# Six of 31 convolution taps as diagonal products on TensorE, compressors in column halves, and a new order of masks, Silus and one low part

## What is computed

```python
CONV_CH, CONV_WIDTH, SEQ = 256, 31, 256
N_Q_HEADS, N_KV_HEADS, HEAD_DIM = 12, 4, 64
CMP_LEN, CMP_STRIDE, CMP_HIDDEN = 32, 16, 256

def conv_mixer(a, w_dw, b_dw, ln_g, ln_b):
    u, v = jnp.split(a, 2, axis=-1)
    y = u * jax.nn.sigmoid(v)
    y = lax.conv_general_dilated(            # each channel alone, 31 taps, causal
        y, w_dw[:, None, :], window_strides=(1,),
        padding=[(CONV_WIDTH - 1, 0)],
        dimension_numbers=("NWC", "WIO", "NWC"),
        feature_group_count=CONV_CH) + b_dw
    y = layer_norm(y, ln_g, ln_b)
    return jax.nn.silu(y)

def compress(kr, pe, w1, w2):                # once for keys, once for values
    b, t = kr.shape[:2]
    chunks = kr.reshape(b, t // CMP_STRIDE, CMP_STRIDE, N_KV_HEADS, HEAD_DIM)
    lo = jnp.einsum("bclgd,ldh->bcgh", chunks, w1[:CMP_STRIDE])
    hi = jnp.einsum("bclgd,ldh->bcgh", chunks, w1[CMP_STRIDE:])
    h = lo[:, :-1] + hi[:, 1:] + jnp.einsum("ld,ldh->h", pe, w1)
    return jnp.einsum("bngh,hd->bngd", jax.nn.silu(h), w2)

def hybrid_layer(x, ...):
    h = rms_norm(x, attn_norm)
    z = h @ w_in                             # u v | q | kc vc ks vs kw vw | gates
    conv_out = conv_mixer(a_conv, conv_w, conv_b, conv_ln_g, conv_ln_b)
    kc = compress(kc_r, ...); vc = compress(vc_r, ...)
    nsa_out = nsa_attention(q, kc, vc, ks, vs, kw, vw, gates)
    x = x + concatenate([conv_out, nsa_out]) @ w_out
    ...                                      # feed-forward, then the second layer
```

## Time and profile before

| what | value |
|---|---|
| median of three executions | 749.86 us |
| the profiled execution: own time / span | 749.76 us / 748.0 us |
| PE busy in the span | 734.2 us (98%) |
| DVE / ACT / POOL busy | 538.5 us (72%) / 377.3 us (50%) / 51.0 us (7%) |
| TensorE clock granted, mean of the span | 0.996 |
| chain that ended last | PE 81%, DVE 12%, ACT 3%, DMA 2% |

### The profile page before, as it was taken

How to read it: one execution, slowest core, us unless ns; L and a number is a source line. 1 busy time by engine, 2 the same in 40 slices (tenths; PEclk the granted TensorE clock), 3 DMA queues, 4 the chain that set the end, 5 groups by cost and what they waited for, 6 DMA issues and landing times.

```text
span 748.0 us, 13134 instructions
## 1 busy us (share of the span) xinstructions
PE 734.2 (98%) x5288; PEld 677.4 (91%) x5288; DVE 538.5 (72%) x927; ACT 377.3 (50%) x544; POOL 51.0 (7%) x72
## 2 busy tenths in 40 slices
PE   8999999999999999999999999999999999999996
PEld 7999987789999999998999999999988998998995
DVE  6798798586677776847669978884967876555554
ACT  7533778664433334446444447665645444444442
POOL 1950000000000000000432000000000000000000
PEclk9999999999999999999999999999999999999999
DMA  8636421479787888642354556554733674644611
GB/s 329 236 117 238 161 65 50 161 307 340 285 317 298 304 323 318 233 161 93 131 195 151 175 198 254 202 188 170 270 124 113 248 258 170 224 168 168 224 57 57
DMA packets 27022, 151.10 MB, mean 202 GB/s; under 512 B 3128, under 2 KB 7836, under 8 KB 9564
## 3 DMA queue, kind: packets, MB, share of 16 engines
q1 hardware_dynamic: 22620, 124.81, 46.1%
q10 hardware_dynamic: 3456, 25.17, 8.5%
q0 software_dynamic: 896, 0.43, 0.3%
HBM read 148.92 MB, written 1.05 MB: 200 GB/s over the span
## 4 chain that ended last, share of the span: by engine, by line
PE 81%; DVE 12%; ACT 3%; DMA 2%; issue 1%; SPq 0%; DVEq 0%; ACTq 0%
PE ps L468 24%; PE ps L469 24%; PE ps L470 24%; DVE ada L1767 4%; DVE w_lo L1671 2%; PE ps L795 2%; PE ps L593 1%; DMA raw<-wts 1%; PE ps L1045 1%; ACT w_hi L1224 1%; DMA raw<-rows_b 1%; PE ps L627 1%; PE ps L617 1%; PE ps L645 1%; PE ps L1031 1%
## 5 line engine op out<-in xcount | busy, mean ns | idle before, releaser
L1671 DVE TENSOR_TENSOR w_lo<-raw,w_hi 128x2048 fp32r<-128x2048 f32 (+2 forms) x105 | 237.5, 2267 | 111.4 <-ACT w_hi L1224 111.1
L468 PE MATMUL ps<-h_hi,w_hi 128*128 128x256 f32 (+2 forms) x984 | 280.1, 285 | 0.0
L469 PE MATMUL ps<-h_lo,w_hi 128*128 128x256 f32 (+2 forms) x984 | 278.3, 283 | 0.0
L470 PE MATMUL ps<-h_hi,w_lo 128*128 128x256 f32 (+2 forms) x984 | 278.3, 283 | 0.0
L1224 ACT CAST w_hi<-raw 128x2048 fp32r<-128x2048 f32 (+2 forms) x105 | 196.8, 1886 | 50.4 <-PE ps L470 46.6
L468 PEld LDWEIGHTS ps<-h_hi,w_hi 128*128 128x128 f32 (+2 forms) x984 | 187.2, 190 | 2.1 <-issue 1.0
L469 PEld LDWEIGHTS ps<-h_lo,w_hi 128*128 128x128 f32 (+2 forms) x984 | 187.2, 190 | 1.2
L470 PEld LDWEIGHTS ps<-h_hi,w_lo 128*128 128x128 f32 (+2 forms) x984 | 187.2, 190 | 0.3
L468 PE MATMUL ps<-w_hi,mix_hi 128*128 128x512 f32 x248 | 97.5, 393 | 0.4 <-DVE w_lo L1671 0.2
L469 PE MATMUL ps<-w_lo,mix_hi 128*128 128x512 f32 x248 | 96.8, 390 | 0.0
L470 PE MATMUL ps<-w_hi,mix_lo 128*128 128x512 f32 x248 | 96.5, 389 | 0.0
(11 more groups left out here) (319 smaller groups left out, 920.2 us busy)
## 6 DMA issues: line engine op xcount, KB each, us to landing
raw<-wts SPq DMA_DIRECT2D x109, 1024.0 KB, 4.8
ada<-w_ada ACTq DMA_DIRECT2D x24, 1024.0 KB, 5.4
alibi<-wts SPq DMA_DIRECT2D x2, 1024.0 KB, 6.7
fa_whole<-wts SPq DMA_DIRECT2D x2, 1024.0 KB, 6.4
resid<-x SPq DMA_DIRECT2D x2, 512.0 KB, 3.8
raw<-wts SPq DMA_DIRECT2D x2, 512.0 KB, 6.8
rows_ga<-rows_wide SPq DMA_DIRECT2D x1, 1024.0 KB, 6.9
out<-resid SPq DMA_DIRECT2D x4, 256.0 KB, 2.0
```

Of the source, the lines that this page charges most:

```text
L468: nc.tensor.matmul(o, lh, rh, start=start, stop=False)
L469: nc.tensor.matmul(o, lh, rl, start=False, stop=False)
L470: return nc.tensor.matmul(o, ll, rh, start=False, stop=stop)
L1671: V.tensor_tensor(w_lo[:, s % RING, 0:w], raw[:, n_of[name] % RAW, 0:w], w_hi[:, s % RING, 0:w].bitcast(F32), ALU.subtract).then_inc(w_rea ...
```

## The change

The change has four parts.

1. The last six taps (25 to 30) of both channel tiles leave DVE. ACT makes twelve diagonal matrices (`tap_diag`: the identity times one column of tap weights, into `rows_ga`, which is free then) ahead of its first copy of a projection. PE multiplies them with the shifted `ypad` behind q1, into bank 7, twelve float32 products of 128 x 128 with 256 columns, and raises `tap_sum_ps`. DVE keeps 50 taps and adds the sum from PSUM to `conv` in one instruction, which now raises `conv_ready`. The taps behind each split are set by a table, 10, 10, 10, 8, 2, 10; the last ten stand behind the low part of vs.
2. A compressor's products are written as column halves: twice 64 columns of the weight block, into partitions 0 to 63 and 64 to 127 of the same PSUM columns, one half behind the other for each j.
3. On ACT the Silu of the keys goes ahead of the copy of the values' sums, and `after(7)`, the high part of vw, goes behind the Silu of the values. On DVE `masked(1)` goes ahead of the mean's subtraction.
4. On DVE `after(7)`, the low part of vw, goes from ahead of `compressor_sum(1)` to behind the copies of the compressed values, ahead of the reciprocal.

```diff
--- before.py
+++ after.py
@@ -82,6 +82,7 @@
 TILES = plan()
 STORED = memory_order()
 CMP_BASE = (0, 48)
+PE_TAPS = 6
 OWN_BANK = {"g": 7, "vs": 6, "vw": 7, "k1": 7}
 G_COLS = 36
 IDX_COLS = 136
@@ -171,6 +172,12 @@
         early = ada[:, :, :].rearrange("p a w -> p (a w)")
         ypad = early[:, 0:572].rearrange("p (c t) -> p c t", c=2)
         conv = early[:, 572:1084].rearrange("p (c t) -> p c t", c=2)
+        on_pe = [(w, c) for c in range(2) for w in range(CONV_W - PE_TAPS, CONV_W)]
+
+        def tap_diag(w, c):
+            i = on_pe.index((w, c))
+            return rows_ga[:, i // 8, (i % 8) * P:(i % 8 + 1) * P]
+
         lnv = early[:, 1084:1596].rearrange("p (a t) -> p a t", a=2)
         lnd = z[:, U, :].rearrange("p (c t) -> p c t", c=2)
         lnq = z[:, V_, :].rearrange("p (c t) -> p c t", c=2)
@@ -262,6 +269,7 @@
         dstep, astep, gstep = sem("dve_step"), sem("act_step"), sem("pool_step")
         zeroed, alibi_ready = sem("zeroed"), sem("alibi_ready")
         conv_ready, conv_mean, convd_ready, conv_var = (sem(n) for n in ("conv_ready", "conv_mean", "convd_ready", "conv_var"))
+        ypad_ready, diag_ready, tapsum_ps = (sem(n) for n in ("ypad_ready", "tap_diagonals_ready", "tap_sum_ps"))
         lnv_ready, lnsq_ready, lnn_ready, chi_ready, clo_ready = (sem(n) for n in (
             "lnv_ready", "lnsq_ready", "lnn_ready", "conv_hi_ready", "conv_lo_ready"))
         kr_ready, cmp_ps, cmp_sb, cmp_sum, cmp_h, cmp2_ps, cmp2_sb, vblk_ready = (sem(n) for n in (
@@ -580,6 +588,13 @@
             i.then_inc(pe_tile, 1)
             for s in range(1, 8):
                 feature_tile(*project_1(s), h_hi, h_lo, 0 if s == 1 else None).then_inc(pe_tile, 1)
+                if s == s_idx["q1"]:
+                    pe.wait_ge(ypad_ready, 1)
+                    pe.wait_ge(diag_ready, 2 * PE_TAPS)
+                    for w, c in on_pe:
+                        i = nc.tensor.matmul(ps[:, 7, c * T:(c + 1) * T], tap_diag(w, c), ypad[:, c, w:w + T],
+                                             start=(w == CONV_W - PE_TAPS), stop=(w == CONV_W - 1))
+                    i.then_inc(tapsum_ps, 1)
 
 
             def compress(a):
@@ -589,9 +604,11 @@
                     landed(pe, name)
                     wc = raw_of(name).rearrange("p (j h) -> p j h", j=8)
                     for f in range(2):
+                        at = slice((2 * half + f) * 66, (2 * half + f + 1) * 66)
                         for j in range(8):
-                            i = nc.tensor.matmul(ps[:, 4 + a, (2 * half + f) * 66:(2 * half + f + 1) * 66], wc[:, j, f * P:(f + 1) * P],
-                                                 kr[a][:, j, :], start=(j == 0), stop=(j == 7))
+                            for e in range(2):
+                                i = nc.tensor.matmul(ps[e * HD:(e + 1) * HD, 4 + a, at], wc[:, j, f * P + e * HD:f * P + (e + 1) * HD],
+                                                     kr[a][:, j, :], start=(j == 0), stop=(j == 7))
                     i.then_inc(direct_done, 1)
 
             def head_at(h):
@@ -1297,6 +1314,10 @@
                 else:
                     nc.scalar.copy(z[:, z_at[name], :], ps[:, bank, :]).then_inc(z_evac, 1)
 
+            act.wait_ge(vec_ready, 2)
+            for w, c in on_pe:
+                nc.scalar.activation(tap_diag(w, c), ident, ACT.Identity, scale=vec_b[:, 2 * w + c:2 * w + c + 1]).then_inc(diag_ready, 1)
+
             for s in range(8):
                 copy_out(s)
                 if s < 7:
@@ -1313,16 +1334,19 @@
 
             act.wait_ge(direct_done, 2)
             nc.scalar.copy(xs_cmp(0), ps[:, 4, 0:264]).then_inc(cmp_sb, 1)
-            attn(0)
-            attn(1)
-            after(7)
-            act.wait_ge(direct_done, 4)
-            nc.scalar.copy(xs_cmp(1), ps[:, 5, 0:264]).then_inc(cmp_sb, 1)
-            for a in range(2):
+            def cmp_silu(a):
                 act.wait_ge(cmp_sum, a + 1)
                 for f in range(2):
                     dst = hcmp[a][:, f, :].rearrange("p (g n) -> p g n", g=NKV)[:, :, 0:N_CMP]
                     nc.scalar.activation(dst, cmp_hidden(a)[:, f], ACT.Silu, bias=pebias[:, 2 * a + f:2 * a + f + 1]).then_inc(cmp_h, 1)
+
+            attn(0)
+            attn(1)
+            cmp_silu(0)
+            act.wait_ge(direct_done, 4)
+            nc.scalar.copy(xs_cmp(1), ps[:, 5, 0:264]).then_inc(cmp_sb, 1)
+            cmp_silu(1)
+            after(7)
             copy_out(s_idx["g"])
             act.wait_ge(cmp2_ps, 1)
             for b in range(2):
@@ -1756,7 +1780,7 @@
             split(2, s_name[2])
 
 
-            taps = [(w, c) for w in range(CONV_W) for c in range(2)]
+            taps = [(w, c) for w in range(CONV_W - PE_TAPS) for c in range(2)]
             base = steps[0]
             def tap(w, c):
                 src, wcol = ypad[:, c, w:w + T], vec_b[:, 2 * w + c:2 * w + c + 1]
@@ -1765,25 +1789,24 @@
                 else:
                     dve.wait_ge(dstep, steps[0] - 1)
                     i = V.scalar_tensor_tensor(conv[:, c, :], src, wcol, conv[:, c, :], ALU.mult, ALU.add)
-                if (w, c) == taps[-1]:
-                    i.then_inc(conv_ready, 1)
-                else:
-                    steps[0] += 1
-                    i.then_inc(dstep, 1)
-
-            behind = 10
+                steps[0] += 1
+                i.then_inc(dstep, 1)
+
+            taps_after = {1: 10, 2: 10, 3: 10, 4: 8, 5: 2, 6: 10}
+            done = 0
             for s in range(7):
                 after(s)
                 if s == s_idx["v"]:
                     dve.wait_ge(z_evac, s + 1)
                     dve.wait_ge(zeroed, 1)
-                    link(V.tensor_tensor(ypad[:, :, CONV_W - 1:], zt(U), zt(V_), ALU.mult))
-                if s >= s_idx["v"]:
-                    a = behind * (s - s_idx["v"])
-                    for w, c in taps[a:a + behind]:
-                        tap(w, c)
-            for w, c in taps[behind * (7 - s_idx["v"]):]:
-                tap(w, c)
+                    V.tensor_tensor(ypad[:, :, CONV_W - 1:], zt(U), zt(V_), ALU.mult).then_inc(ypad_ready, 1)
+                    dve.wait_ge(ypad_ready, 1)
+                for w, c in taps[done:done + taps_after.get(s, 0)]:
+                    tap(w, c)
+                done += taps_after.get(s, 0)
+            dve.wait_ge(dstep, steps[0])
+            dve.wait_ge(tapsum_ps, 1)
+            V.tensor_tensor(conv, conv, ps[:, 7, :].rearrange("p (c t) -> p c t", c=2), ALU.add).then_inc(conv_ready, 1)
 
 
             def compressor_sum(a):
@@ -1834,12 +1857,11 @@
             compressor_sum(0)
 
             masked(0)
+            masked(1)
             dve.wait_ge(conv_ready, 1)
             dve.wait_ge(conv_mean, 1)
             link(V.tensor_tensor(lnd, conv, ps[:, 6:7, 0:T].to_broadcast([P, 2, T]), ALU.subtract))
             V.tensor_tensor(lnq, lnd, lnd, ALU.mult).then_inc(convd_ready, 1)
-            masked(1)
-            after(7)
             compressor_sum(1)
             dve.wait_ge(conv_var, 1)
             V.tensor_scalar(lnv[:, 0, :], ps[:, 6, T:2 * T], EPS, None, ALU.add).then_inc(lnv_ready, 1)
```

## The result

The changed kernel takes 752.06 us in the median (749.73 to 754.48), the kernel before 749.87 in the same comparison: 1.0032 times as long, 95% interval 1.0019 to 1.0045. I had predicted 749.8 us and no difference. The time lies in the range, 0.14 us under its upper end; that the change makes the kernel slower was not the forecast. The profiled execution took 752.73 us, its span is 750.4 us (before: 749.76 and 748.0).

The account below looks back on a forecast made before the run. Bound: the chain of waits through E, the end of DVE's layer-norm product. E = 72.67 + 2C, plus copies 2.99, low part 2.20 and 3.87 from reciprocal to product, 89.23 against 89.20: no change, 749.8 us, range 748.0 to 752.2.

Parts of the forecast that it names:

- Taps on PE, 5.42 us: Twelve float32 tap products on PE behind q1 take 5.42 us uncovered, so the first compressor starts at 63.49.
- The tap sum ready at about 67.3, no gap before the mean: DVE raises `conv_ready` at about 67.3, as before; PE reaches the mean at 68.8, so its 0.72 us gap goes.
- C: Time of one compressor on PE: 3.75 us with column halves running together, against 7.19 or 7.09 before.
- E: End of the layer norm's product on DVE, taken to set the kernel's end: 89.23 forecast, 89.20 before.
- Rival 1: Compressor halves load and stream in turn: C 7.0 to 7.2, 6.5 to 6.9 us more, 756.5 us; chance 0.12.
- The other 7.60 are PE's own (...) and stay: From the mean's start to the copies of values, PE's 7.60 us besides one compressor stay unchanged.
- rival 2: Compressor halves run together but are fed too slowly: C 5.1, E 91.9, 752.5 us; chance 0.10.
- The low part's 2.20 us on the path: Low part of vw on DVE, now between copies and reciprocal, costs its full 2.20 us on the way to E.
- Rival 3: Low part of vw on DVE doesn't count, PE's gain gets through: E 87.0, 747.6 us; chance 0.11.
- Rival 4: Fourth compressor tile loads late, at 7.3 us per load: PE loses 1.1 us, 750.9; chance 0.07.
- PE gains 2.2 us up to the projection vs, and waits them off again: PE reaches the projection vs 2.2 us earlier, then waits before the transposes at 101.39; costed at nothing.

Follow-up runs that it names:

- k1: Changed kernel with the low part of vw moved from between copies and reciprocal to right behind DVE's EPS addition to the variance: 750.09 us.
- the second trace: The changed kernel run and traced once more without any edit: 753.20 us median, 1.0036 to 1.0062 times the kernel before.
- k11: Changed kernel plus 192 extra PE wait instructions ahead of the compressors and four unread products in PE's gap before the second transposes: 750.22 us.

## Why the prediction was wrong

- **Taps on PE, 5.42 us: right.** The twelve products take 5.35 us in after, and the compressor starts at 63.76 instead of 63.49. The diagonals on ACT took 3.66 us, inside my bounds, and nobody waited for them.
- **The tap sum ready at about 67.3, no gap before the mean: right.** It ends at 67.50.
- **C = 3.75: close.** It is 3.90, which makes 0.3 us of E. Rival 1, halves in turn, falls: 256 loads and products run in 3.9 us, 0.061 us for each two halves. The Trainium skill, TensorE: Matmul & The Clock Gate, section The mechanism, has the rule that a load overlaps a running product only where the row group differs. This trace does not agree: with both halves over the same 128 rows, loads and products take the same 3.9 us side by side.
- **"The other 7.60 are PE's own (...) and stay": one of the two steps that failed.** From the mean to the copies, less one compressor, it is 82.40 - 69.17 - 3.90 = 9.33 us in after, of which 1.39 are the stop. I asked in rival 2 whether PE can issue 256 loads and products in 3.75 us, and priced that by the pair. Issuing was no limit; whether the next block of instructions is there in time, as the records of the five stops suggest it was not, I did not ask. That rival 2's 752.5 us is next to the 752.06 measured is luck: it comes from a C of 5.1, which did not come.
- **The low part's 2.20 us on the path: right**, 2.21 in the trace, and 1.97 of the time by k1. The time's share is not clean, since k1 also takes PE's wait away behind which the clock falls; the 2.07 by which E moves are the low part's alone. Rival 3 falls. Rival 4 is not seen: PE doesn't wait for a compressor's tile in after.
- **E = 89.23: 91.48 in the first trace, 89.26 in the second.** The 2.25 in the first are 0.27 from the start, 0.30 from C, 1.55 from the stop by the starts of its two products, and 0.13 that is not traced. In the second the start is 0.79 earlier, and C (0.30), the stop (0.39) and the same 0.13 make up for it: that E comes out right there is luck, since before, from which the 63.49 was worked out, had the fall of the clock ahead of the stage and the second trace had not.
- **"PE gains 2.2 us up to the projection vs, and waits them off again": the other step that failed.** The gap came as forecast, and I costed it at nothing because PE only waits there. Where the clock falls behind it, it costs 1.6 to 2.9 us. In the second trace E is no later than forecast, and a loss of 2.9 us is there all the same.

With both costs taken away by the two additions of k11, the change takes 750.22 us, 0.4 over the 749.8 predicted and 0.7 over before. The 0.27, 0.30 and 0.13 above add up to as much.

## What to carry to other kernels

Where an edit splits instructions, count them as well as their time: an engine that uses up a block of instructions in a quarter of the time it took before can stand still, here for 0.4 to 1.7 us, at an instruction that has nothing to do with the edit. And idle time on TensorE that seems free has to be looked at for what the granted clock does behind it, in more than one trace. Work that was hidden in a wait should stay in it: moving the low part onto the path cost 2.1 to 2.2 us of E and opened the gap behind which the clock falls.

## What the runs showed of the hardware

- Two products of 66 columns on 64-column halves of the array, over the same 128 rows, run side by side with their loads: 128 pairs of records in 3.90 us instead of 64 in 7.1.
- Instructions come in blocks of 16 KB, by the estimate above 256 of PE's, and PE went on 2.2 to 2.5 us behind the start of a block's record in the five traces with a stop. One kernel showed 1.39 us of idle time in one trace and 0.23 in another.
- The granted clock fell to 0.50, for 3.4 or 6.8 us, within 1.6 us behind the end of PE's wait before the transposes, in four of the six traces where that wait is 1.95 to 1.98 us, and at that place in none of eight where the longest was 0.7.
